# The first dense tile's gates, added word by word into a zeroed DRAM matrix by GpSimd in place of one-hots and products

## The reference, cut to what matters

```
q = (xb @ w_pq).reshape(-1, 8, 2, 128)                    # 8 heads, 2 halves
sc = einsum('thpd,hpkd->thpk', q, sub_keys)               # 128 keys a half
v1, i1 = top_k(sc[:, :, 0], 16);  v2, i2 = top_k(sc[:, :, 1], 16)
top_sc, pos = top_k(v1 + v2 over all 256 pairs, 16)       # 16 experts a head
eidx = i1 * 128 + i2 at pos;  gate = softmax(top_sc)
hid = gelu(einsum('td,thkd->thk', xb, u_tab[eidx]))
out = einsum('thk,thkd->td', gate * hid, v_tab[eidx])     # + residual
```

## Time and profile before

| | us |
|---|---|
| median of 3 runs | 1772.53 (1771.45 to 1777.73) |
| the profiled execution, its own time | 1774.21 |
| its span, first to last instruction | 1771.7 |
| PE busy | 1660.0 (94%) |
| DVE busy | 1209.8 (68%) |
| GpSimd busy | 695.7 (39%) |
| ACT busy | 365.1 (21%) |
| moved by DMA | 552.61 MB, mean 312 GB/s |

### The profile page before, as it was taken

How to read it: one execution, slowest core, us unless ns; L and a number is a source line. 1 busy time by engine, 2 the same in 40 slices (tenths; PEclk the granted TensorE clock), 3 DMA queues, 4 the chain that set the end, 5 groups by cost and what they waited for, 6 DMA issues and landing times. The chain is left out here.

```text
span 1771.7 us, 19797 instructions
## 1 busy us (share of the span) xinstructions
PE 1660.0 (94%) x6994; PEld 1229.4 (69%) x6994; DVE 1209.8 (68%) x2606; ACT 365.1 (21%) x906; POOL 695.7 (39%) x601
## 2 busy tenths in 40 slices
PE   7998999999778998799889999999999999999987
PEld 6887888877665786687776666666666666566633
DVE  2252112697899778899987998677666666656676
ACT  1041123125321244634750001101000000000101
POOL 0000000132324438622765655545544546544542
PEclk9998999999889999899999999999999999999999
DMA  5532543675757959997999999999999999999997
GB/s 190 184 101 95 167 142 119 230 256 191 249 191 271 389 167 351 350 322 231 367 336 409 406 409 409 409 406 410 404 409 409 406 410 407 387 409 410 409 379 279
DMA packets 224337, 552.61 MB, mean 312 GB/s; under 512 B 15696, under 2 KB 112080, under 8 KB 223600
## 3 DMA queue, kind: packets, MB, share of 16 engines
q0 software_dynamic: 82944, 302.03, 44.4%
q1 hardware_dynamic: 118304, 237.69, 36.7%
q10 hardware_dynamic: 22992, 11.64, 2.2%
HBM read 534.22 MB, written 16.42 MB: 311 GB/s over the span
## 5 line engine op out<-in xcount | busy, mean ns | idle before, releaser
L786 POOL DMA_INDIRECT M<-in_u_tab,IDX x288 | 334.6, 1162 | 709.0 <-DVE PEER L1731 341.1
L793 POOL DMA_INDIRECT M<-in_v_tab,IDX x288 | 357.0, 1240 | 342.0 <-DVE X L1752 264.3
L1076 PE MATMUL PSB<-XN,M 128*128 128x256 f32 x2048 | 463.6, 380 | 8.0 <-ACT M L1298 4.5
L1084 PE MATMUL PSB<-M,HST 128*128 128x512 f32 x1024 | 460.7, 595 | 7.0 <-DMA M<-in_v_tab 3.4
L1076 PEld LDWEIGHTS PSB<-XN,M 128*128 128x128 f32 x2048 | 389.0, 191 | 107.4 <-issue 52.6
L1731 DVE CUSTOM_DVE_ANT_0 M<-M,XN 128x1024 f32<-128x1024 f32 x288 | 351.3, 1221 | 125.2 <-DMA M<-in_u_tab,IDX 117.8
L1752 DVE SCALAR_TENSOR_TENSOR X<-M,PEER,X 128x1024 f32<-128x1024 f32 x256 | 328.0, 1281 | 98.3 <-DMA M<-in_v_tab,IDX 84.5
L835 PE MATMUL PSB<-M 128*128 128x256 f32 (+1 forms) x1536 | 366.5, 400 | 6.8 <-DVE M L1386 6.1
L835 PEld LDWEIGHTS PSB<-M 128*128 128x128 f32 x1536 | 297.0, 195 | 67.8 <-DVE M L1386 7.0
L1084 PEld LDWEIGHTS PSB<-M,HST 128*128 128x128 f32 x1024 | 194.4, 191 | 210.5 <-issue 195.4
L842 PE MATMUL PSB<-M 128*128 128x256 f32 (+1 forms) x928 | 211.4, 387 | 1.1 <-ACT M L1262 0.7
(11 more groups left out here) (213 smaller groups left out, 1085.4 us busy)
## 6 DMA issues: line engine op xcount, KB each, us to landing
M<-in_u_blocks SPq DMA_DIRECT2D x128, 512.0 KB
M<-in_v_tab SPq DMA_DIRECT2D x128, 512.0 KB
M<-in_w_in SPq DMA_DIRECT2D x24, 1024.0 KB
M<-in_w_pq SPq DMA_DIRECT2D x16, 1024.0 KB
gate_spill<-M ACTq DMA_DIRECT2D x11, 1024.0 KB, 17.7
M<-gate_spill SPq DMA_DIRECT2D x16, 704.0 KB
M<-in_w_out SPq DMA_DIRECT2D x8, 1024.0 KB
M<-in_w_mq SPq DMA_DIRECT2D x8, 1024.0 KB
```

The costliest lines, as they stand in the source:

```text
L786: pool.indirect_dma_start(out=UA[:, s % RR, :], out_offset=None, in_=utab, in_offset=bass.IndirectOffsetOnAxis(ap=IDX[:, n:n + 1], axis=0) ...
L793: pool.indirect_dma_start(out=VA[:, s % RR, :], out_offset=None, in_=vtab, in_offset=bass.IndirectOffsetOnAxis(ap=IDX[:, n:n + 1], axis=0) ...
L1076: last = pe.matmul(PSB[:, 4 + b % 2, 0:2 * P], UBLK[:, b % SR, c, :], XN[:, 1:3, c * P:(c + 1) * P], start=(c == 0), stop=(c == DC - 1))
L1084: last = pe.matmul(PSB[:, 2 * t + hf, :], WR[:, b % WRING, t * P:(t + 1) * P], VBLK[:, b % SR, hf * 512:(hf + 1) * 512], start=(b == 0), s ...
```

## The change

Tile 1's gates no longer pass through one-hots and products.

- DVE zeroes 1,024 columns of SBUF (`ZERO`) at the start, and SP writes them to the first eight chunks of `gate_spill` in 16 transfers of 512 KB, two behind each of eight early weight loads.
- When tile 1's keys are known, DVE works out for each token and chosen expert the word's index in `gate_spill` (`SIDX`), by pairs of heads. The softmax of tile 1 is made by pairs of heads too (four parts in place of one).
- GpSimd adds the gates into that tensor with 128 indirect transfers with an add, each of 128 single words (one for each token), two behind the fetches of each slot from slot 28 on. Ahead of every 16th it waits until all before it have landed.
- `tt(1)`, 32 batches of `oh` and `gb`, and tile 1's eight chunk transfers are gone.
- Scores of tile 2 and 4 go into the buffers of tiles 0 and 1 (`SCA`), so that `HR` is free from the start, and ACT's waits in `lk` go.
- The plan: 26 in place of 29 for `G0_SLOTS` (three slots fewer ahead of the sweep), 14 of the `lk` merged with the rest of the routing and ring work before tile 2's `tt`, 2 there, 6 among tile 2's one-hots, none behind them. Of the late routing of tile 2, two pieces of three go first, where it was one of two.
- SP issues the first two gate groups at `w(0)`, where it did behind `lk(14)`, and waits there for all scatters.

```diff
+SCATTERS = NK
+SCATTER_SLOT = 28
+SCATTERS_A_SLOT = 2
+SCATTER_US = 1.0
+GROUP_STRIDE, KEY_STRIDE = P * NSP * GRP * CH_TOK, NSP * GRP * CH_TOK
...
-G0_SLOTS = 29
+G0_SLOTS = 26
+AHEAD_RT = 14
+AHEAD_OH = 6
+LATE_TURNS = 3
...
+def routed_by_pairs(t):
+
+    s, held = [], []
+    for pair in range(PH // 2):
+        pieces = rt(t, pair)
+        s += pieces[:2] + held + pieces[2:] + soft(t, pair)[:1]
+        held = soft(t, pair)[1:]
+    return s + held
...
-    second = [x for pair in range(PH // 2) for x in rt(1, pair)] + soft(1)
+    second = routed_by_pairs(1)
     extra = first[:7] + merged(first[7:], slots[:one]) + merged(second, slots[one:early])
-    extra += [("tt", 1)] + merged(batches(1), slots[early:mid])
+    extra += slots[early:mid]
...
-            t_dve += dve_us(x)
+            t_dve += dve_us(x) + SCATTER_US * (x[0] == "d" and SCATTER_SLOT <= x[1] * TOPK + x[2] < SCATTER_SLOT + SCATTERS // SCATTERS_A_SLOT)
...
-    out += merged(late, extra) + merged(rt(2, 3), ahead[:3])
-    out += soft(2)[:1] + late_slots[:2] + ahead[3:4] + soft(2)[1:] + late_slots[2:4] + ahead[4:5] + [("tt", 2)]
+    out += merged(merged(late + rt(2, 3), extra), ahead[:AHEAD_RT])
+    ahead = ahead[AHEAD_RT:]
+    out += soft(2)[:1] + late_slots[:2] + ahead[:1] + soft(2)[1:] + late_slots[2:4] + ahead[1:2] + [("tt", 2)]
+    ahead = ahead[2:]
...
-        g0 += [("oh", 2, k), ("oh", 2, k + 1)] + ahead[5 + k * 10 // n:5 + (k + 2) * 10 // n]
+        g0 += [("oh", 2, k), ("oh", 2, k + 1)] + ahead[k * AHEAD_OH // n:(k + 2) * AHEAD_OH // n]
...
-    out += merged(g0, late_slots[4:-22]) + merged(ahead[15:], late_slots[-22:-10])
+    out += merged(g0, late_slots[4:-22]) + merged(ahead[AHEAD_OH:], late_slots[-22:-10])
...
+            sp.wait_ge(zero_set, 1)
...
+                if NW < i <= NW + 8:
+                    for k in range(2 * (i - NW - 1), 2 * (i - NW)):
+                        sp.dma_start(spill[k, :, 0:FIRST_STAGED, :], ZERO.rearrange("p (c x) -> p c x", c=FIRST_STAGED)).then_inc(zeroed, 16)
...
-                if seg == ("lk", HRING - 8):
+                if seg == ("w", 0):
...
+                    sp.wait_ge(scattered, 16 * SCATTERS)
...
+            gates = spill.rearrange("k p c (x one) -> (k p c x) one", one=1)
+
+            def scatter(n):
+
+                if n == 0:
+                    pool.wait_ge(zeroed, 16 * NBLK // GRP)
+                if n % (2 * TOPK) == 0:
+                    pool.wait_ge(gates_done, softs_before(DENSE[0], n // (2 * TOPK)) + 1)
+                if n and n % TOPK == 0:
+                    pool.wait_ge(scattered, 16 * n)
+                pool.indirect_dma_start(out=gates, out_offset=bass.IndirectOffsetOnAxis(ap=SIDX[:, n:n + 1], axis=0),
+                                        in_=GATE[:, DENSE[0], :, :].rearrange("p h k -> p (h k)")[:, n:n + 1], in_offset=None,
+                                        compute_op=ALU.add).then_inc(scattered, 16)
...
+                    if i * TOPK + s >= SCATTER_SLOT:
+                        for _ in range(min(SCATTERS_A_SLOT, SCATTERS - nscatter)):
+                            scatter(nscatter)
+                            nscatter += 1
...
+                if (t, b4) == (1, 0):
+                    act.wait_ge(zeroed, 16 * NBLK // GRP)
+                if (t, b4) == (2, 0):
+                    wait_routed(act, 0)
+                if (t, b4) == (NP, 0):
+                    wait_routed(act, 1)
...
             def const():
+                dve.memset(ZERO, 0.0).then_inc(zero_set, 1)
+                dve.wait_ge(const_ok, 2)
+                dve.tensor_copy(TOKEN[:, 0:1], TOKEN_I[:, 0:1]).then_inc(token_step, 1)
+                dve.tensor_scalar(TOKEN_I[:, 1:2], TOKEN_I[:, 0:1], CH_TOK.bit_length() - 1, None, ALU.logical_shift_right).then_inc(token_step, 1)
...
-                    if t in DENSE:
-                        dve.tensor_copy(I12[:, t - 1, :, 2 * TOPK * pair:2 * TOPK * (pair + 1)], EQS).then_inc(topk_done, 1)
+                    if t == DENSE[1]:
+                        dve.tensor_copy(I12[:, :, 2 * TOPK * pair:2 * TOPK * (pair + 1)], EQS).then_inc(topk_done, 1)
+                    elif t == DENSE[0]:
+                        part = SPART[:, 1, :]
+                        dve.tensor_scalar(SHIGH, EQS[:, 0, :], GRP.bit_length() - 1, None, ALU.logical_shift_right).then_inc(place_step, 1)
+                        dve.tensor_scalar(part, EQS[:, 0, :], float(CH_TOK), TOKEN[:, 1:2], ALU.mult, ALU.add).then_inc(place_step, 1)
```

More of the change, by code:

```diff
@@ L182, in merged @@
             nb += 1
[L183 to L191, removed]
     return s
@@ L212, in plan @@
     first = [x for pair in range(PH // 2) for x in rt(0, pair)] + soft(0)
-    second = [x for pair in range(PH // 2) for x in rt(1, pair)] + soft(1)
+    second = routed_by_pairs(1)
     extra = first[:7] + merged(first[7:], slots[:one]) + merged(second, slots[one:early])
-    extra += [("tt", 1)] + merged(batches(1), slots[early:mid])
+    extra += slots[early:mid]
     late_slots, slots = slots[mid:last], slots[last:]
     t_pe = t_dve = 0.0
-    gone, held, late, odd = set(out), [], [], 0
+    gone, late, odd = set(out), [], 0
     for w in work:
[L221 to L224, removed]
         while (extra or late) and w[0] in LONG and t_dve < t_pe:
             odd += 1
-            if late and (odd % 2 or not extra):
+            if late and (odd % LATE_TURNS or not extra):
                 out.append(late.pop(0))
@@ L297, in hot_places @@
     at, last, turn = {}, {}, 0
-    for seg in PLAN:
-        if seg == ("a1", NP):
-            free = PLAN.index(seg)
     for n, seg in enumerate(PLAN):
         if seg[0] == "oh":
-            places = [0, 1] if n < free else [0, 1, 2] if seg[1] == DENSE[0] else [0, 1, 3, 4]
+            places = [0, 1, 3, 4]
             place = places[turn % len(places)]
@@ L327, in jobs_of @@
         return [(seg, "A")]
-    if k == "gb" and seg not in SMALL:
-        return [(seg, "A")]
-    if k in ("dt", "o", "mo") or seg == ("tt", 1):
+    if k in ("dt", "o", "mo"):
         return [(seg, "D")]
@@ L1051, in gb @@
             def gb(t, n):
-                m = DENSE.index(t) * P // OH_TOK + n
-                if ("gb", t, n) not in SMALL:
-                    bank = open_job(("gb", t, n))
-                else:
-                    settle()
-                    bank = small_bank()
-                    if t == DENSE[1] and n == 0:
-                        pe.wait_ge(tt_out, 1)
-                pe.wait_ge(oh_done, m + 1)
+                settle()
+                bank = small_bank()
+                if n == 0:
+                    pe.wait_ge(tt_out, 1)
+                pe.wait_ge(oh_done, n + 1)
                 for j in range(OH_TOK):
                     last = pe.matmul(bank[:, j * P:(j + 1) * P], hot_buffer(t, n)[:, j, 1, :], hot_buffer(t, n)[:, j, 0, :], start=True, stop=True)
-                if ("gb", t, n) not in SMALL:
-                    done(last)
-                else:
-                    last.then_inc(oh_used, 1)
+                last.then_inc(oh_used, 1)
             def lk(b):
@@ L1300, in oh @@
             def oh(t, n):
-                d = DENSE.index(t)
-                m, c = d * P // OH_TOK + n, n * OH_TOK
-                act.wait_ge(hot_done, m + 1)
+                c = n * OH_TOK
+                act.wait_ge(hot_done, n + 1)
                 for j in range(OH_TOK):
                     first = hot_buffer(t, n)[:, j, 0, :]
-                    last = act.activation(first, first, ACT.Copy, scale=TT[:, d, 2, c + j:c + j + 1])
+                    last = act.activation(first, first, ACT.Copy, scale=TT[:, 2, c + j:c + j + 1])
                 last.then_inc(oh_done, 1)
@@ L1778, in oh @@
             def oh(t, n):
-                d = DENSE.index(t)
-                m, c = d * P // OH_TOK + n, n * OH_TOK
-                if n == 0 and d == 0:
-                    wait_drained(dve, ("tt", 1))
-                if n == 0 and d == 1:
+                c = n * OH_TOK
+                if n == 0:
                     dve.wait_ge(tt_out, 1)
                 place, before = HOT[t, n]
-                if place == 2 and not before:
-                    wait_job(dve, ("s", NP, 1))
                 if place >= 3 and not before:
```

138 lines of the change are left out of this document (63 added, 75 removed).

## The result

The changed kernel takes 1850.12 us (median of 4 runs, 1846.49 to 1853.82) against 1772.53 us for the kernel before on the same chip: ratio 1.0438, 95% interval 1.0411 to 1.0465. A fourth run of the kernel before took 4473.5 us and is left out of these numbers. The prediction, 1757 us and faster, has the wrong sign, and the time lies outside its range of 1738 to 1804 us.

What follows compares the result with a forecast made beforehand. Bound: a PE, DVE and GpSimd braid before the sweep, then PE and DMA both full. 1774.2 - 34 + 1 + 10 (GpSimd late) + 7.7 (moved slots) = 1758.9, 1757 us at the median; range 1738 to 1804.

Steps and rivals of the forecast that it cites:

- I take 1.35: GpSimd ahead of the sweep: each of 128 scatters costs 1.35 us; with 28 us of waits, a need of 201 us.
- 1.72 us: GpSimd's price for a gather over the whole stretch, used as the dear price of a scatter: need 248 us.
- a room of 191: GpSimd's idle time between fetches 28 and 92, 189 + 22 - 20 = 191 us; only need beyond it delays the start.
- the sign did not turn at 1.47 us: Prediction put break-even at a scatter price of 1.47 us on GpSimd, 216 us of need, 25 us of lateness.
- What comes off and the start without GpSimd: Before the sweep: PE loses 42 us of work, DVE 40; less PE's gap, the sweep starts 34 us earlier.
- The head: Kernel start: DVE's memset of 1,024 columns (about 1.0 us) and three small operations delay PE by 1 us.
- The waits for landing: GpSimd waits seven times for its scatters to land, 4 us each, 28 us in all.
- The DMA engines: Rival: 18,432 small packets no longer fit above 67 ns each; 1845 us at 152 ns; chance 0.07. Forecast took 27 ns, hidden.
- The moved slots: Three ring slots moved into the sweep bring 3.1 MB of gathers under a full DMA: 7.7 us later.
- GpSimd becomes the bound: Rival: before the sweep, scatters at 1.72 us need 57 us more than the room; 1804 us, slower; chance 0.22.
- DVE held up by more GpSimd instructions: Shared SBUF port: 128 more GpSimd instructions would also hold up DVE; set aside, no size given.
- The lower end of the range: 1738 us, from the rival that GpSimd keeps up everywhere (chance 0.20), with the 42 us bound on the earlier start.

Runs made afterwards that it cites:

- experiment 4: Kernel before plus 36 extra indirect transfers in GpSimd's idle time at the start, six of a kind (words and rows; added, written, gathered): 1769.57 us.
- experiment 3: Changed kernel with scatters that write the word in place of adding it, same number, indices and waits: 1806.0 us, ratio 1.0193 to the kernel before.
- experiment 2: Changed kernel with only its first 64 scatters, one a slot in place of two: 1775.69 us, ratio 1.0022 to the kernel before.
- experiment 1: Changed kernel without its 128 scatters and the waits for them, all else kept: 1754.92 us, ratio 0.9913 to the kernel before.
- experiment 6: Kernel before with `G0_SLOTS` 26 in place of 29 and nothing else changed: 1774.56 us, ratio 1.0017.
- (5): Changed kernel with three scatters a slot in place of two and `G0_SLOTS` 16 in place of 26: 1884.02 us, ratio 1.0635 to the kernel before.

## Why the prediction was wrong

**The step that failed is "I take 1.35", the price of a scatter on GpSimd.** It was the gather's price between a clean and a busy stretch. Measured: 2.12 us, 0.77 more, 128 x 0.77 = 98 us. Some 0.6 of it is the add (experiment 4: 1.55 against 0.96 and 0.94; experiment 3: means of 1.82 and 1.21). The rest is that these instructions take longer in the full stretch than alone, a mean of 1.82 us (median 1.62) against 1.55, and by more than the 0.1 us over the clean gather that I had allowed; no run takes apart what stretches them. I had noted that no row shows a transfer that adds, and still bounded its price above by the price of gathers, 1.72 us. That bound excluded what happened: it was a bound on contention, not on the unknown operation. By the prediction's own sum with the measured need, 271 + 12 = 283 us less a room of 191 gives 92 us late, and -33 + 92 + 7.7 = +67 of the 80.4 us.

**A second step failed, and by the estimate below it was enough to turn the sign: that GpSimd's idle time is a room that can be filled for nothing.** The size of the room was nearly right: without scatters GpSimd waits 199.6 us for DVE, where I had 191 (the gathers got 17.5 us shorter for the 22 taken, the stretch 7.5 for the 20). The three loads measured, scatters with their gaps and waits, against the start without any: 117.7 + 19.1 + 3.4 = 140 us of load cost 12.0 us (experiment 2), 154.9 + 38.3 + 11.5 = 205 us cost 46.0 (experiment 3), 283 us cost 96.3. By a room of 191 they would have cost 0, 14 and 92. On a line between the first two, the 201 us that I predicted would have cost about 44, and the whole -27.5 + 44 + 9 = +25 us: slower at my own price too. To break even the load may cost 27.5 - 9 = 18.5 us of start, about 152 us of load by the same line, (152 - 12) / 128 = 1.1 us a scatter. That is under the 0.94 + 0.30 of the cheapest indirect transfer that any run here shows. So by this estimate the sign did not turn at 1.47 us, and 128 of these transfers had no price at which they paid. It is an interpolation, not a measurement: experiment 2 changes the number a slot as well as the total, and its 12.0 comes from the shortest of its executions; by the medians of the runs the first two costs are 20.8 and 51.1, which leaves still less room.

The other steps, in the prediction's order:

- *What comes off and the start without GpSimd:* 34 us taken, bounds 28 and 42, with the head 33 (27 to 41); measured 27.5 with the head (experiment 1), at the lower bound. PE's gap ahead of the first `vd` is 14.75 us there, on DVE's ring work behind the last one-hot, as argued, and at the long end of the 6 to 15 taken; PE's 42 us less this gap is 27.3. With the scatters the gap is 18.05 us.
- *The head:* the memset of 1,024 columns took 0.91 us for the predicted 1.0.
- *The waits for landing:* 28 us taken, 12.1 measured, in five waits.
- *The DMA engines:* q0 shows exactly 18,432 packets more. Its share of 45.7% of 1852.1 us against 44.4% of 1771.7 is 60 us x 16 / 18,432 = 52 ns a packet, between the 27 of the spills and the 67 that would have been too much. That rival falls: the DMA share in the stages of loss is 0.72 to 0.75, and the gathers do not land late. The rule weighed with it, from the Specifications section of DMA: Bandwidth & Descriptors in the Trainium skill, on transfers below 512 bytes, is not refuted by this: twice the spill's price a packet is in its direction, but it did not decide.
- *The moved slots:* 7.7 us taken; 7.2 (experiment 6), 8.6 (1) and 2.5 a slot over ten slots (5). In the changed kernel the time from the first `vd` on is 11.6 longer; the 3 us over experiment 1 are not explained.
- *The rival "GpSimd becomes the bound"* was right in mechanism, place and signs: DVE waits for gathers, and PE stands still for 38 us ahead of tile 2's `tt`. Its price, 1804 us, was too small, mostly by the add.
- *DVE held up by more GpSimd instructions*, the rule weighed and set aside, does not show: DVE's dots and adds of `v` rows have means of 1.222 and 1.282 us, and 1.221 and 1.281 before.
- *The lower end of the range:* the sum for the bound of 42 us gives 1739 with the head's 1 us, and 1738 without it.

## What to carry to other kernels

When a change hands an operation that no row shows to an engine, price it by a short experiment or leave its upper bound open; the bound from the nearest operation covers only what the two have in common. Idle time of an in-order engine on which others depend is worth less than its sum: here 12 to 21 us were lost when seven tenths of it were filled. And where single words are scattered to DRAM, the count of transfers decides what GpSimd pays, and the spacing of the words what the DMA engines pay.

## What the runs showed of the hardware that was not expected

- An add in an indirect transfer costs GpSimd about 0.6 us an instruction for words (1.55 us against 0.96) and about 0.5 for rows of 4 KB (1.55 against about 1.1). On 64 partitions the adding instruction takes 1.42 us. The section SWDGE vs HWDGE vs iDMA of DMA: Bandwidth & Descriptors in the Trainium skill says that GpSimd builds the descriptors in software and that only its transfers can accumulate; the time that both take it is what these rows show for this case, and no run here tried an add from another queue.
- An adding scatter of 128 words makes 144 packets, a writing one 32.
- Adds to words beside each other take the DMA engines much longer than words 512 bytes or more apart: 11 to 17 us against 2.4 to 4.2 until six have landed. With 128 of them between the gathers the DMA engines stood at a share of 0.99 while moving 187 GB/s. Over 128 scatters this was 122 us of the kernel's time, and by q0's shares (50.1% of 1995.6 us less 44.4% of 1771.7, times 16, over 18,432) 185 ns a packet against 52 to 53. Which part of the memory or of the engines makes them wait was not tried, nor whether plain writes pay the same (six to words beside each other took 7.8 us to land).
